# Two decoder layers on one core: from a loop over layers to one block with counting semaphores, with an early request for the next layer's weights and a store by tiles

## The reference, cut to what matters

```python
p = x @ w_in                                   # 1024 -> N_IN columns, split among three mixers
o = concat(fox(p), nsa(rope(p)), dsa(rope(p))) # 16 heads of 64
x = layer_norm(ALPHA * x + o @ w_out)          # first sub-layer
s = sigmoid(x @ w_router)                      # 64 experts, top 8 of 4 groups
y = sum_e gate_e * down_e(silu(x @ gate_e) * (x @ up_e)) + shared(x)
x = layer_norm(ALPHA * x + y)                  # second sub-layer
```

## Time and profile before

| | |
|---|---|
| median of 3 runs | 1330.5 us (1330.44 to 1330.78) |
| the profiled execution | 1334.92 us |
| its span | 1333.1 us |
| PE busy | 1244.2 us (93%) |
| DVE / ACT / POOL busy | 544.9 / 346.6 / 135.3 us |
| moved by DMA | 454.61 MB, mean 341 GB/s |

### The profile page before, as it was taken

How to read it: one execution, slowest core, us unless ns; L and a number is a source line. 1 busy time by engine, 2 the same in 40 slices (tenths; PEclk the granted TensorE clock), 3 DMA queues, 4 the chain that set the end, 5 groups by cost and what they waited for, 6 DMA issues and landing times. The chain is left out here.

```text
span 1333.1 us, 26928 instructions
## 1 busy us (share of the span) xinstructions
PE 1244.2 (93%) x10810; PEld 662.0 (50%) x10810; DVE 544.9 (41%) x1581; ACT 346.6 (26%) x721; POOL 135.3 (10%) x196
## 2 busy tenths in 40 slices
PE   7998989999999999999589889899999999999993
PEld 7985853434344443343279758443433543343331
DVE  3768363333322323233447774533332322323324
ACT  4647321111111111111145573111111111111111
POOL 1571120000000000000025612100000000000000
PEclk9998999999999999999889999999999999999996
DMA  7471389999999999999363805899999999999992
GB/s 276 159 301 48 140 342 407 422 422 421 422 421 420 421 421 421 421 423 422 117 226 130 345 2 218 329 418 422 422 421 421 421 420 421 421 421 422 422 416 78
DMA packets 60486, 454.61 MB, mean 341 GB/s; under 512 B 4336, under 2 KB 5104, under 8 KB 6000
## 3 DMA queue, kind: packets, MB, share of 16 engines
q1 hardware_dynamic: 60400, 453.40, 82.7%
HBM read 452.34 MB, written 1.05 MB: 340 GB/s over the span
## 5 line engine op out<-in xcount | busy, mean ns | idle before, releaser
L805 PE MATMUL bank<-expert_weights,gathered 128*64 128x512 f32 x2048 | 456.8, 596 | 13.2 <-DMA expert_weights<-in_moe_w 11.2
L805 PEld LDWEIGHTS bank<-expert_weights,gathered 128*64 128x64 f32 x2048 | 140.9, 137 | 325.0 <-issue 293.2
L823 PE MATMUL bank<-expert_weights,hT 128*32 128x512 f32 x2048 | 233.0, 595 | 2.5 <-DVE hT L1496 2.5
L1491 DVE TENSOR_TENSOR sig<-sig,bank 128x256 f32<-128x256 f32 x64 | 26.9, 421 | 352.3 <-ACT sig L1101 352.2
L1111 ACT ACTIVATE y_hi<-bank,gate_slot 128x512 fp32r<-128x512 f32 x128 | 88.1, 688 | 308.7 <-PE bank L823 308.7
L1501 DVE SCALAR_TENSOR_TENSOR y_lo<-bank,gate_slot,y_hi 128x512 fp32r<-128x512 f32 x128 | 96.1, 750 | 172.6 <-ACT y_hi L1111 172.6
L1101 ACT ACTIVATE sig<-bank 128x256 f32<-128x256 f32 x64 | 24.6, 384 | 422.0 <-PE bank L805 422.0
L823 PEld LDWEIGHTS bank<-expert_weights,hT 128*32 128x32 f32 x2048 | 60.6, 109 | 139.6 <-issue 139.6
L464 PE MATMUL bank<-piece_hi,x_hi 128*128 128x256 f32 x416 | 121.3, 292 | 0.0
L784 PEld LDWEIGHTS bank<-hot,x_part 128*128 128x128 bf16 x3072 | 93.2, 98 | 54.3 <-issue 50.7
L465 PE MATMUL bank<-piece_lo,x_hi 128*128 128x256 f32 x416 | 117.6, 283 | 0.0
(11 more groups left out here) (194 smaller groups left out, 1148.3 us busy)
## 6 DMA issues: line engine op xcount, KB each, us to landing
expert_weights<-in_moe_w SPq DMA_DIRECT2D x192, 2048.0 KB, 21.9
piece<-in_pieces SPq DMA_DIRECT2D x35, 1024.0 KB, 5.1
shared_weights<-in_ws SPq DMA_DIRECT2D x2, 3072.0 KB, 13.1
ln_rows<-in_lnw SPq DMA_DIRECT2D x4, 1024.0 KB, 9.1
x_sb<-in_x SPq DMA_DIRECT2D x1, 1024.0 KB, 4.8
out<-x_sb SPq DMA_DIRECT2D x1, 1024.0 KB, 4.0
router_w<-in_router SPq DMA_DIRECT2D x2, 256.0 KB, 4.9
upper<-in_const_upper SPq DMA_DIRECT2D x1, 256.0 KB, 6.6
```

What stands on the lines that cost most here:

```text
L805: mm = pe.matmul(C[e * PAIR:(e + 1) * PAIR, :], xgT[par][:, d, e * PAIR:(e + 1) * PAIR], W[:, e, d * 2 * EF:(d + 1) * 2 * EF], start=(d == ...
L823: mm = pe.matmul((A, B)[c][to:to + SLOTS, :], hT[:, f, of_:of_ + SLOTS], W[:, e, EGU + f * D + c * 512:EGU + f * D + (c + 1) * 512], start ...
```

## The change

1. **One block, no loop.** Each engine's program holds both layers, one after the other (`for layer in range(DEPTH)` in Python). No semaphore is cleared between layers: `sem(name, in_a_layer)` notes how far a semaphore rises in a layer, and `at(s, n)` adds that number times the layer to the value waited for. The clears and the barrier are gone. The rare path for overfull experts has semaphores of its own for each layer.
2. **Next layer's pieces early.** After the last expert loads SP requests piece 0 (in two halves) and piece 1 once the last pair's gate/up is done, piece 2 once the last pair's hidden values are turned, pieces 3 and 4 once `combined` is full. For that `hotT`, `hT`, `y_hi`, `y_lo` and `sig` lie in other slots of the ring. The overflow flag is read by SP before that.
3. **Layer 1's start is interleaved.** ACT casts piece 2 before the layer norm's square roots and piece 3 after them. PE turns token tile 0, multiplies the first half of its `project(0)`, turns tile 1, and does the rest.
4. **x loaded turned.** The host lays x out turned as `x_t`; two DMAs of 512 KiB bring it into `xT`. Piece 0 comes in two halves between them. PE starts with the first halves. The turning of x on PE and ACT is gone at the start. x in rows (`x_sb`) is loaded after piece 4. The constants are loaded between the pieces: `misc` and `upper` after piece 3. `ones` is gone. DVE waits for all five constants before it copies the masks and before x_lo.
5. **Output by tiles.** Token tile 0 is stored when it is normalised, tile 1 in two halves of 512 columns; the last tile's `affine` works on 512 columns at a time.

The core of the diff:

```diff
+        def at(s, n, layers_back=0):
+
+            return s, n + (here[0] - layers_back) * per_layer[s]
...
+                    if layer == 0:
+                        for g in range(2):
+                            sp.dma_start(xT[:, 4 * g:4 * g + 4, :], x_t[:, 4 * g:4 * g + 4, :]).then_inc(x_ld[g], 16)
+                            load_first(0, 0, g).then_inc(first_piece[g], 16)
+                        load_first(0, 1).then_inc(piece_ld[1], 16)
+                        for dst, src in ((ident[:, :], consts["ident"]),
+                                         (rope_cs[:, :, :, :], consts["rope"]), (cmask_f[:, :], consts["cmask"])):
+                            sp.dma_start(dst, src).then_inc(once, 16)
+                        for n in (2, 3):
+                            load_first(0, n).then_inc(piece_ld[n], 16)
+                        for dst, src in ((misc_c[:, :], consts["misc"]), (upper[:, :, :], consts["upper"])):
+                            sp.dma_start(dst, src).then_inc(once, 16)
+                        load_first(0, 4).then_inc(piece_ld[4], 16)
...
-                    sp.wait_ge(combined, 2 * TT)
+                    sp.wait_ge(*at(routed_ready, 1))
                     more = sp.value_load(flag[0:1, 0:1], min_val=0, max_val=1)
...
+                        if layer + 1 < DEPTH:
+                            sp.wait_ge(*at(main.gu, 2 * PAIRS))
+                            for g in range(2):
+                                load_first(layer + 1, 0, g).then_inc(first_piece[g], 16)
+                            load_first(layer + 1, 1).then_inc(piece_ld[1], 16)
+                            sp.wait_ge(*at(main.ht_ps, PAIRS))
+                            load_first(layer + 1, 2).then_inc(piece_ld[2], 16)
+                            sp.wait_ge(*at(combined, 2 * TT))
+                            for n in (3, 4):
+                                load_first(layer + 1, n).then_inc(piece_ld[n], 16)
...
+                for t in range(TT):
+                    for c in range(1 + t):
+                        cols = slice(c * 512, (c + 1) * 512) if t else slice(0, D)
+                        sp.wait_ge(*at(ln_done, TT + 1 + t + c))
+                        sp.dma_start(out[0, t * P:(t + 1) * P, cols], x_sb[:, t, cols]).then_inc(stored, 16)
+                sp.wait_ge(stored, 16 * 3)
...
+                    def project_first(t, g):
+
+                        for k in range(4 * g, 4 * g + 4):
+                            mm = pe.matmul(ps_proj(0, t), xT[:, k, t * P:(t + 1) * P], piece[0][:, k, :], start=(k == 0), stop=(k == KD - 1))
+                        if g == 1:
+                            mm.then_inc(proj, 1)
...
+                        turn_normalised(0)
+                        for g in range(2):
+                            pe.wait_ge(*at(first_piece[g], 16))
+                        pe.wait_ge(*at(xt_sb, 5, 1))
+                        project_first(0, 0)
+                        turn_normalised(1)
+                        pe.wait_ge(*at(xt_sb, 6, 1))
+                        project_first(0, 1)
+                        for g in range(2):
+                            pe.wait_ge(*at(xt_sb, 7 + g, 1))
+                            project_first(1, g)
...
+                    if layer > 0:
+                        act.wait_ge(*at(main.dn, 2 * PAIRS, 1))
+                        split_hi(2)
+                        deviation(3, (0, 1), 1)
+                        split_hi(3)
+                        for t in range(TT):
+                            copy_xT(act, 4, t, (bank[4 + 2 * t], bank[5 + 2 * t]), 1)
...
+                    if layer == 0:
+                        dve.wait_ge(once, 16 * 5)
+                        own.mark(V.tensor_copy(identb[:, :], ident[:, :]))
+                        for a in range(2):
+                            own.mark(V.tensor_copy(cmask[:, a, :], cmask_f[:, :]))
+                        own.settle()
+                        dve.nop().then_inc(masks_ready, 1)
                     for g in range(2):
-                        dve.wait_ge(xhi_ready, g + 1)
+                        dve.wait_ge(*at(xhi_ready, g + 1))
                         V.tensor_tensor(x_lo[:, 4 * g:4 * g + 4, :], xT[:, 4 * g:4 * g + 4, :], x_hi[:, 4 * g:4 * g + 4, :].bitcast(F32), ALU.subtract).then_inc(xlo_ready, 1)
...
-            for n, s in enumerate(names):
-                engines[n % len(engines)].sem_clear(s)
-            nc.all_engine_barrier()
```

More of the change, by code:

```diff
@@ L111, in restart, with build @@
         self.n = 0
-def build(nc, x, pieces, rows, small, moe_w, ws, router, lnw, consts, out):
+def build(nc, x, x_t, pieces, rows, small, moe_w, ws, router, lnw, consts, out):
     ctx = ExitStack()
@@ L203, in build @@
         hot = [place(f"hot{s}", [P, TT, 2, SLOTS], BF16, where=moe_at) for s in range(2)]
-        hotT = [place(f"hotT{s}", [P, P], F32R, where=moe_at) for s in range(2)]
         assert moe_at[0] <= ring_at + LAST_IN_SLOT * SLOT
@@ new lines, in _ @@
+                for t in range(TT):
[4 more added lines that the diff above has]
+                sp.wait_ge(stored, 16 * 3)
+            @block.tensor
+            def _(pe):
+                for layer in range(DEPTH):
+                    here[0] = layer
+                    over, over_ld = overs[layer], over_lds[layer]
@@ L903, in _, with deviation @@
                         pe.nop()
-                    for t in range(TT):
-                        normalised(pe, 1, t)
-                        turn_x(pe, xt_ps, t, (bank[4 + 2 * t], bank[5 + 2 * t]))
-                @block.scalar
-                def _(act):
-                    own = Order(act, act_own)
+            @block.scalar
+            def _(act):
+                own = Order(act, act_own)
+                for layer in range(DEPTH):
+                    here[0] = layer
+                    over = overs[layer]
+                    def deviation(count, tiles, layers_back=0):
+                        act.wait_ge(*at(ln_var, count, layers_back))
+                        for t in tiles:
+                            act.activation(ln_s[:, t, 19:20], ln_s[:, t, 15:16], ACT.Sqrt).then_inc(ln_rs, 1)
                     def read_plain(c):
                         for t in range(TT):
-                            act.wait_ge(proj, 2 * c + t + 1)
+                            act.wait_ge(*at(proj, 2 * c + t + 1))
                             ps, slot = ps_proj(c, t), (2 * c + t) % 4
@@ L1183, in _ @@
                         pool.nop().then_inc(split_c, 1)
-                    pool.wait_ge(sh_gate, 1)
-                    pool.wait_ge(sh_up, 2 * TT)
+                    pool.wait_ge(*at(sh_gate, 1))
+                    pool.wait_ge(*at(sh_up, 2 * TT))
                     G.tensor_tensor(shT[:, :, :], shS[:, :, :], shT[:, :, :], ALU.mult).then_inc(sh_h, 1)
-                @block.vector
-                def _(dve):
-                    own = Order(dve, dve_own)
-                    V = nc.vector
+            @block.vector
+            def _(dve):
+                own = Order(dve, dve_own)
+                V = nc.vector
+                for layer in range(DEPTH):
+                    here[0] = layer
+                    over = overs[layer]
                     def rotate(c, tiles=range(TT)):
@@ L1567, in _ @@
                     for t in range(TT):
-                        affine(1, t)
-                    own.settle()
-            engines = (nc.sync, nc.scalar, nc.vector, nc.tensor, nc.gpsimd)
-            for n, s in enumerate(names):
-                engines[n % len(engines)].sem_clear(s)
-            nc.all_engine_barrier()
-        with nc.Block() as block:
-            @block.sync
-            def _(sp):
-                sp.dma_start(out.rearrange("b (t p) d -> p (b t) d", p=P), x_sb[:, :, :]).then_inc(stored, 16)
-                sp.wait_ge(stored, 16)
+                        affine(1, t, 512 if layer == DEPTH - 1 and t == TT - 1 else D)
 def shape_constants():
```

530 lines of the change are left out of this document (267 added, 263 removed).

## The result

| | before | after |
|---|---|---|
| median of the runs on one chip | 1331.03 us (6 runs, 1330.44 to 1335.04) | 1320.95 us (6 runs, 1318.48 to 1324.78) |
| ratio, 95% interval | | 0.9924 [0.9904, 0.9944] |
| span of the profiled execution | 1333.1 us | 1318.7 us |

The kernel became faster by 10.1 us, where 18.2 had been forecast; 1320.95 lies above the range. The profiled executions differ by 14.4 us. So there are two questions: why 14.4 and not 18.2, and why the runs show 10.1 where their own profiled executions show 14.4.

What follows compares the result with a forecast made beforehand. Weight streaming bounds the first expert stage and PE's order the front, so only PE's idle places can gain: 11.0 + 7.8 - 0.65 = 18.2 us. Median 1330.5 to 1312.3 us, range 1307 to 1318.5 (about 0.82).

Steps and rivals of the forecast that it cites:

- the start: Start of the execution: first three-product matmul 1.85 us earlier, less 2.5 for a fall of the clock: -0.65 us.
- between the layers: From layer 0's last add-back to layer 1's `project(2)`: PE goes on without clears, barrier and jump, 11.0 us gained.
- the end: After the last affine: no transposes, copies, clears or barrier before a smaller last store, 7.8 us gained.
- the change of the low-clock spells in the two fronts: In either layer's front, spells may vanish or grow as all is shifted: 1305 to 1308.5 us; chance 0.09.
- PE's walk: Between the layers: PE's steps from turning tile 0 until 661.3 to `project(2)` at 677.4, where before had 688.43.
- rival (b): ACT's early casts delay the layer norm, or constants landing at 19 make DVE late: 1316.5 to 1319 us; chance 0.12.
- the jump's share: Between the layers: part of 4.18 us of issue is the loop's jump stalling instruction fetch, and goes with the barrier.
- the first MiB lands at 0.75 + 4.8: At the start: first halves of x_t and piece 0 land at 5.55, so PE starts at 5.6.
- low clock at the start: PE's first two projections take 14.0 us plus about 2.3 for a low clock, and end at 21.9.
- the median of the runs, which is 4.4 below it: Step from the profiled execution, forecast at 1316.7 us, to the median of the runs, 1312.3.
- Rival (d): The gain between the layers isn't passed on through the expert stream, only the end gains: 1322.7 us; chance 0.05.
- (e): Expert loops: waits with the layer's offset need two more register instructions each, making it slower, 1341 us; chance 0.03.

Runs made afterwards that it cites:

- the filled start: The changed kernel with 12 extra matmuls, results unused, in the first layer's gap before the first three-product matmul: 1318.02 us, 0.9902 of before.
- the last kernel: The kernel "all together" with 40 more extra matmuls on PE during the layer norm between the layers: 1310.09 us, 0.985 of before.
- all together: The changed kernel with all constants before pieces 2 and 3, x_t and piece 0 in whole DMAs, 21 extra matmuls per front: 1313.46 us, 0.9865.

## Why the prediction was wrong

The sum was worked out from one execution, and it had terms for three places only: the start, between the layers, and the end. These came to 17.3 us of the 18.2 in the profiled executions (10.4 + 7.3 - 0.4). What failed is the term that it put at nothing, the change of the low-clock spells in the two fronts, and with it the step from the profiled execution to the median of the runs, in which the same spells come and go.

**Between the layers: right.** 10.4 us of 11.0. PE's walk held to 0.6 us, the late square roots of rival (b) didn't come in this kernel (0.22 us were left), and piece 2's low part was ready 25.8 us after the last add-back (674.30 + 2.25 - 650.79) where 25.2 had been forecast. The walk rests on the interleaved start and on pieces that are there early; the experiments show that neither is needed for the gain. Without the early request it is 28.7 us, without the interleaving 29.0, each taken away alone. What remains for the gain is the clears, the barrier and the jump with what they kept apart; no run puts these back, so this is by elimination.

The prediction cited the Trainium skill (Runtime: NRT & Kernel Launch, Instruction fetch mechanics) for the jump's share. The trace agrees that no stall of issue is left between the layers; no run here parts the jump from the barrier.

**The end: right.** 7.3 us of 7.8. The last store took 2.0 us (2.1 forecast; the 2.6 that the prediction sets beside it was further off), and from the last affine to the end it is 2.5 (2.6 forecast). The last affine itself ends 13.4 us after the last add-back's row at 1302.83, and 12.6 in the kernel before: the split last tile takes 2.98 instead of 2.59 us, and DVE starts on the add-back 0.37 us later.

**The start: its sum came out by luck, its terms were wrong.** Forecast: matmul at 25.2 and a fall of the clock for 2.5, so 27.7 against 27.07, a loss of 0.65. Measured: 27.46 and a fall that cost 1.5, so a loss of 1.9. That start and first front together lost only 0.5 us is luck: the later spell of the first front was 3.4 us shorter than in before, which the sum didn't have. The step that failed here is "the first MiB lands at 0.75 + 4.8", so at 5.55: in halves PE could start only at 7.57, and the 2 us went down the queue to the constants (19.12 instead of 17.1). Whole loads give them back (17.33). So the condition of rival (b), constants at 19, came true, without the time it named for it. That the clock falls in PE's wait was right; the fall came at 27.9, behind waits of 0.39, 1.04 and 1.95 us. The prediction's "low clock at the start" of PE isn't in the record, which shows 1.00 there; PE did run at half its rate (last section). The constants' place in the queue is worth 4.7 us in the means, more than halves or wholes (1.8 us at the first three-product matmul).

**The clock in the fronts: the step that failed first.** The forecast took the low-clock spells as they were in before and gave their change 0.09, in the direction of a gain. In the profiled executions the later spell of the first front shrank and that of the second grew: the second front is 1.9 us longer, with 6.8 us of low clock instead of 3.2. It isn't that PE waits more. The timelines of PE show the same two waits ahead of the place, before and then after:

```profile
738.99 0.44 PE L502 MATMUL bank<-ident,hq 128*128 128x128 f32 x2 [0.72 <-DVEq L1214]
...
747.24 0.40 PE L570 MATMUL bank<-kcT,qkT 64*128 64x15 f32 x4 [0.86 <-ACTq L954]
```

```profile
730.19 0.44 PE L522 MATMUL bank<-ident,hq 128*128 128x128 f32 x2 [0.72 <-DVEq L1287]
...
738.43 0.40 PE L590 MATMUL bank<-kcT,qkT 64*128 64x15 f32 x4 [0.86 <-ACTq L1012]
```

They stand 51 and 59 us behind the layer's first three-product matmul in both. In after the clock falls 2.9 us behind the second; in before it stays up there and falls later, behind a wait of 1.91 us at 782. With fillers in these waits and in the one of 1.91 us neither kernel's clock falls in its fronts, and the two kernels' means lie 14.85 us apart, not 10.5. So the spells do hang on these waits. What decides whether a given wait brings a spell was not found. In the kernel with the filled start, whose second layer is that of after, the same two waits brought none.

**From the profile to the median: the larger part.** The forecast carried the span to the runs by "the median of the runs, which is 4.4 below it". That was taken as something which the change leaves alone. It was this execution: before's profiled span is 2.7 us above its mean, after's 1.2 below. After's spread follows the clock: its 12 spans go from 1316.7 us at a mean granted clock of 0.985 to 1323.0 at 0.981, and in the last kernel an execution at 0.991 has 1314.7, one at 0.996 1306.8. Before's does so less well: among its executions are 1326.9 us at 0.982 and 1330.5 at 0.983. The half rate at the start, which the clock's record doesn't show, can be part of that: the trace of before with fillers has 1.7 us less of it than before's. No short execution of before was traced, so where its 2.7 us lie stays open.

So the 8.1 us between 18.2 and 10.1 are: 3.9 from the profiled execution to the typical one; 1.9 in the second front, clock; 0.6 between the layers and 0.5 at the end; 1.1 in the first expert stage, against 0.2 gained in the second; and the start with its front 0.15 better than forecast. That is 7.65, and the rest is the difference between medians and means. The 3.9 us are no cause of their own. If the three places are worth 17.3 us in every execution, as in the profiled ones, then the 10.5 us of the means say that the fronts and the expert stages lost 6.8, and the fillers in the fronts bring back 4.35 of these, give or take 2.5. What the rest is stays open. The 1.1 us of the first expert stage are within what the three traces of before and its filled form show of each other (467.3 to 468.6), and are left unexplained. Rival (d), that the gain isn't passed on, and (e), slower register work in the pairs (43 us), are out: the stages kept their length within 1.1 us. The range of (b), "1316.5 to 1319", was the nearest; its late constants came, but the runs lie above it, by the clock in the fronts.

## What to carry to other kernels

Before a profiled execution stands for the runs, compare its span and its granted clock with those of the others: here 4 us of an 8 us miss were in that one step. Where PE has waits like the ones shown here in a stretch, give the low clock that may follow a term in the sum (0.4 us for each us at the low level here), and try a handful of filler matmuls on both versions before judging an edit by a per cent. For before it also made the spans steadier (a standard deviation of 0.9 instead of 1.9 us); for after it didn't (2.1 with, 1.9 without). Look at what stands ahead of the constants in the first queue: moving up 291 KB that DVE needed was worth more than the choice between halves and wholes for the first loads, and the halving only lost time. And take parts of a change away one at a time: of five parts here, the early request and the interleaving brought nothing that shows.

## What was not expected of the hardware

- At the start of the execution PE ran at half its rate although the granted clock is shown as 1.00. In the kernel "all together" the first 32 matmul records took 9.80 us and the next 32 took 7.07, and the slices from 9 to 14 us show 4 matmuls in each us at 1.00, from 15 on 6 or 7. So in the first 15 us the recorded clock doesn't tell PE's rate. It isn't the same in each execution: the 64 records of the first two projections took 15.74 us in the trace of before and 14.05 in that of before with fillers, which has hardly any of it.

```profile
9.00:10.00 1.00, 1.00 (x4) 1.00 0.95 385
...
15.00:16.00 1.00, 1.00 (x7) 1.00 1.00 418
```

- Two tensors read in alternating halves at the start ran at 156 to 305 GB/s for 5 us; the same tensors whole ran at 343 GB/s from 2.75 us and at 372 to 462 from 3.3 on. Two halves of piece 0 between the layers, requested while the stream was still running, landed 4.6 us after their issue.
- A spell at the low clock lasted up to 13.6 us with PE busy all the while (14.00 of 14 us from 88 to 102, at 0.52).
- Fillers that do little for the kernel before (0.9989, 1.2 us of mean span) take 5.5 us off the kernel after: the same means has another worth in two kernels whose fronts do the same work.
